# Stick-breaking attention beside seven projection slabs: the suffix sums and the value products one slab later

## What is computed

```python
z = jnp.einsum("bhqd,bhkd->bhqk", q_blk, k_blk).astype(jnp.float32) * scale
log_not = jnp.where(mask, jax.nn.log_sigmoid(-z), 0.0)
suffix = lax.cumsum(log_not, axis=3, reverse=True) - log_not
log_w = jax.nn.log_sigmoid(z) + suffix
att = jnp.where(mask, jnp.exp(log_w), 0.0)
outs.append(jnp.einsum("bhqk,bhkd->bhqd", att.astype(v.dtype), v_blk))
...
p = p + mu.astype(f32) * (prev - p)
xw = p[..., o:o + DECAY_LORA]; o += DECAY_LORA
xa = p[..., o:o + ICLR_LORA]; o += ICLR_LORA
xg = p[..., o:o + GATE_LORA]; o += GATE_LORA
log_decay = -DECAY_SCALE * jax.nn.sigmoid(w0 + jnp.tanh(xw) @ w_lora)
a = jax.nn.sigmoid(a0 + xa @ a_lora)
g = jax.nn.sigmoid(xg) @ g_lora
```

## Time and profile before

| | |
|---|---|
| median of 3 runs | 1669.34 us (1667.26 to 1671.3) |
| the profiled execution, its own time | 1670.32 us |
| its span in the trace | 1667.9 us |
| TensorE matmuls busy | 1633.1 us, 98% of the span |
| VectorE busy | 1239.9 us, 74% |
| ScalarE busy | 922.4 us, 55% |
| granted TensorE clock, mean | 0.995 of full |

### The profile page before, as it was taken

How to read it: one execution, slowest core, us unless ns; L and a number is a source line. 1 busy time by engine, 2 the same in 40 slices (tenths; PEclk the granted TensorE clock), 3 DMA queues, 4 the chain that set the end, 5 groups by cost and what they waited for, 6 DMA issues and landing times.

```text
span 1667.9 us, 29552 instructions
## 1 busy us (share of the span) xinstructions
PE 1633.1 (98%) x12590; PEld 1497.5 (90%) x12590; DVE 1239.9 (74%) x1358; ACT 922.4 (55%) x1015; POOL 37.5 (2%) x40
## 2 busy tenths in 40 slices
PE   8999999999999999999999999999999999999997
PEld 7988998999999998888999988888888897988887
DVE  6677877975788888776697787657876678677655
ACT  5376534544566557554576655448555456555445
POOL 0000000100000000000020000000000000000000
PEclk9999999999999999999999999999999998999999
DMA  8524445453454544555633455553555541445551
GB/s 295 185 90 169 160 143 202 153 206 122 158 197 181 201 161 167 202 195 187 212 133 127 165 212 188 181 198 130 201 199 189 169 177 72 167 179 184 189 187 54
DMA packets 84136, 287.14 MB, mean 172 GB/s; under 512 B 5856, under 2 KB 54112, under 8 KB 56384
## 3 DMA queue, kind: packets, MB, share of 16 engines
q1 hardware_dynamic: 79984, 273.70, 46.6%
q0 software_dynamic: 2816, 10.69, 1.8%
q10 hardware_dynamic: 1232, 1.25, 0.2%
HBM read 281.42 MB, written 4.19 MB: 171 GB/s over the span
## 4 chain that ended last, share of the span: by engine, by line
PE 86%; DVE 7%; ACT 3%; issue 1%; DMA 1%; POOL 0%; ACTq 0%; DVEq 0%; POOLq 0%
PE PS L476 86%; DVE arena L2151 2%; DVE ring_lo L2148 2%; ACT arena L1484 1%; DVE arena L2148 1%; ACT ring_hi L1484 1%; DMA arena<-spilled_gates 1%; DMA residual<-in_x_t 0%; ACT L1484 0%; ACT operand L1484 0%; DVE arena L2308 0%; DMA ring_raw<-in_w_stream 0%; DVE inv L2207 0%; DVE residual L2148 0%; PE PS L922 0%
## 5 line engine op out<-in xcount | busy, mean ns | idle before, releaser
L476 PE MATMUL PS<-operand,ring_hi 128*128 128x256 f32 (+1 forms) x4360 | 905.6, 329 | 12.7 <-DVE operand L2213 10.2
L476 PEld LDWEIGHTS PS<-operand,ring_hi 128*128 128x128 f32 x4360 | 727.6, 191 | 80.3 <-DVE ring_lo L2148 8.1
L2148 DVE TENSOR_TENSOR ring_lo<-ring_raw,ring_hi 128x2048 fp32r<-128x2048 f32 (+2 forms) x267 | 601.8, 2257 | 203.6 <-ACT ring_hi L1484 203.1
L1484 ACT ACTIVATE ring_hi<-ring_raw 128x2048 fp32r<-128x2048 f32 (+2 forms) x267 | 497.2, 1863 | 192.3 <-PE PS L476 184.7
L476 PE MATMUL PS<-operand,ring_lo 128*128 128x256 f32 x3060 | 601.9, 283 | 0.1
L476 PEld LDWEIGHTS PS<-operand,ring_lo 128*128 128x128 f32 x3060 | 479.9, 192 | 12.0 <-DVE ring_lo L2148 0.4
L1484 ACT ACTIVATE arena<-PS 128x512 f32<-128x512 f32 (+2 forms) x141 | 89.7, 642 | 175.9 <-PE PS L476 164.0
L476 PE MATMUL PS<-hidden,ring_hi 128*128 128x512 f32 x704 | 174.8, 396 | 0.0
L476 PEld LDWEIGHTS PS<-hidden,ring_hi 128*128 128x128 f32 x704 | 128.0, 188 | 26.2
L2148 DVE TENSOR_TENSOR arena<-arena,PS 128x512 f32<-128x512 f32 (+4 forms) x147 | 99.6, 683 | 28.0 <-ACT arena L1484 21.6
L1484 ACT ACTIVATE arena<-arena 128x512 f32<-128x512 f32 (+6 forms) x124 | 85.4, 702 | 59.8 <-DVE arena L2151 32.8
(11 more groups left out here) (160 smaller groups left out, 1125.0 us busy)
## 6 DMA issues: line engine op xcount, KB each, us to landing
ring_raw<-in_w_stream SPq DMA_DIRECT2D x215, 1024.0 KB, 4.8
ring_raw<-in_w_stream SPq DMA_DIRECT2D x64, 512.0 KB, 4.4
ring_raw<-in_w_stream SPq DMA_DIRECT2D x52, 256.0 KB, 3.5
spilled_gates<-arena POOLq DMA_DIRECT2D x12, 256.0 KB, 2.7
arena<-spilled_gates POOLq DMA_DIRECT2D x2, 1536.0 KB, 9.8
tables<-in_tables POOLq DMA_DIRECT2D x1, 1344.0 KB, 9.7
residual<-in_x_t ACTq DMA_DIRECT2D x4, 256.0 KB, 7.7
arena<-in_mem_t POOLq DMA_DIRECT2D x1, 1024.0 KB, 16.6
```

Of the source, the lines that this page charges most:

```text
L476: return nc.tensor.matmul(out, lhs, rhs, start=start, stop=stop, skip_group_check=True)
L1484: return nc.scalar.activation(out, in_, func, **kw)
L2148: return v.tensor_tensor(out, a, b, op)
```

## The change

On TensorE the suffix and value steps of both sets stand one slab later: scores 0, slab 0, scores 1, slab 1, slab 2, suffix 0, slab 3, suffix 1, slab 4, values 0, slab 5, values 1, slab 6. On ScalarE the exponential of set 1 moves behind shift 2 and the split of slab 6, and the operand's high half from turn j = 4 to turn j = 5, behind the split of gate slab 2. On VectorE the addition and mask of set 0 move behind shift 0, the split of slab 4 and take 2, and those of set 1 behind take 3, shift 2 and the split of slab 6. No instruction is added or removed.

```diff
             pe.wait_ge(sem("output_taken"), taken[0] - 2)
-            for j, (part, q) in enumerate(((sb_scores, 0), (sb_scores, 1), (sb_suffix, 0), (sb_suffix, 1),
+            for j, (part, q) in enumerate(((sb_scores, 0), (sb_scores, 1), (None, 0), (sb_suffix, 0), (sb_suffix, 1),
                                            (sb_values, 0), (sb_values, 1))):
-                part(q)
+                if part is not None:
+                    part(q)
                 rwkv_slab(j)
-            rwkv_slab(6)
...
             attention(0)
             shift(1)
             split_slab(START["rwkv"] + 5)
-            attention(1)
             for j in range(2, 7):
                 shift(j)
                 if j < 6:
                     split_slab(START["rwkv"] + j + 4)
-                if j == 4:
+                if j == 2:
+                    attention(1)
+                if j == 5:
                     act.wait_ge(sem("sb_y"), 1)
                     operand(XH[:, 12:16], tiles_of(0, 4))
...
             logs(1)
-            attention(0)
             shift(0)
             split_slab(START["rwkv"] + 4)
             take_rwkv(2)
-            attention(1)
+            attention(0)
             shift(1)
             split_slab(START["rwkv"] + 5)
             for j in range(3, 7):
...
                 if j < 6:
                     split_slab(START["rwkv"] + j + 3)
+                if j == 3:
+                    attention(1)
                 if j == 5:
                     dve.wait_ge(sem("sb_y"), 1)
                     operand(XL[:, 12:16], tiles_of(0, 4), XH[:, 12:16])
```

## The result

| | before | changed |
|---|---|---|
| median of 20 runs each | 1669.66 us (1667.16 to 1672.56) | 1672.8 us (1667.55 to 1674.87) |
| the profiled execution, its own time | 1670.32 us | 1672.69 us |
| its span | 1667.9 us | 1670.1 us |
| TensorE matmuls busy | 1633.1 us | 1634.5 us |

The ratio is 1.0019 (95% interval 1.0013 to 1.0026): slower by about 3.1 us, clear of noise and just inside the 0.2% that was called no change. The forecast was plus 1.15 us. The two profiled executions differ by 2.37 us, their spans by 2.2 us, and the larger part of that can be followed in the traces.

The account below looks back on a forecast made before the run. TensorE was taken as the bound, busy 1633.1 of 1667.9 us. Minus 1.82, plus 3.2, minus 0.23 made plus 1.15 us, set on the 1669.34 us median: 1670.5 us, range 1667.4 to 1673.6 us.

Parts of the forecast that it names:

- A: The forecast case: the wait moves from the suffix sums to the lora products, 1670.5 us (1670.3 to 1671.2); chance 0.60.
- B: Rival: TensorE's clock falls to half in the new wait before the lora products, 1672.9 to 1673.9 us; chance 0.22.
- The old stall: TensorE's wait before the suffix sums of set 1, for VectorE's addition of set 0: taken as gone, minus 1.82 us.
- Rival D: The addition of set 0 comes late, so the wait before the suffix sums isn't removed: up to 1672.3 us; chance 0.06.
- The queue of ScalarE: The operand's activation behind gate slab 2's split delays the lora products: TensorE waits 3.2 us instead of 0.23 us.
- The lora transfer: The lora weights' load on GpSimd's queue, released by VectorE's subtraction: taken as hidden, 0.35 us as upper end.
- the argument against B: The 1.82 us stall at 107.86 us left the clock at full, and dense work stands on both sides.
- B's price: Loss at half clock: 3.4 us for up to 6.8 us at half rate, 2.4 us if only through the lora products.
- The sum behind the lora products: Later chains each start about 1.1 us later; nothing takes the delay up or adds to it.
- The term of A: The sum of the stall removed and the lora wait added, at full clock: plus 1.15 us.
- Rival C: The gain stays, by a shorter path to the lora products or later slack: TensorE keeps 1.82 us, 1667.5 us; chance 0.12.

Follow-up runs that it names:

- e1: The changed kernel, but ScalarE makes the operand's high half in turn 5 ahead of the split of gate slab 2: 1667.23 us, ratio 0.9983.
- e2: The kernel before, with only the operand's high half moved on ScalarE from turn 4 to turn 5, behind the split of gate slab 2: 1675.91 us.
- e4: The changed kernel, but GpSimd loads the lora weights early, when slab 5 is multiplied: 1674.28 us, ratio 1.0028.
- e8: The kernel before, with only shift 6 on ScalarE moved ahead of the split of gate slab 2: 1667.28 us, ratio 0.9992.
- e9: The changed kernel measured once more, nothing altered: 1671.41 us, ratio to before 1.0015.
- e11: A repeat of e5, nothing altered: 1665.18 us, ratio to before 0.9977.
- e10: A repeat of e1, nothing altered: 1667.54 us, ratio to before 0.9993.
- e6: The changed kernel, but TensorE multiplies the first half of gate slab 1 in the wait before the lora products: 1669.65 us, ratio 1.0003.
- e5: The kernel of e1, with shift 6 on ScalarE also moved ahead of the split of gate slab 2: 1665.04 us, ratio to before 0.9975.
- e7: The kernel of e1 plus 13 unused matmuls of 64 columns between gate slab 0 and the lora products: 1670.57 us, ratio to before 1.0012.
- e3: The changed kernel plus 13 unused matmuls of 512 columns between gate slab 0 and the waits before the lora products: 1673.65 us, ratio 1.0025.

## Why the prediction was right, and where it wasn't

The time came out as no change and inside the stated range, but not by the case that set it: A ended at 1671.2 us, the median is 1672.8 us, and what happened is B. With a ratio of 1.0019 against a border at 1.002, "no change" was close to luck.

**The old stall.** Right: VectorE's addition ended at 113.18 us (forecast 113.46), TensorE came to the sums at 113.52 us (113.75), and the wait is gone. Rival D is out. Slab 6 ended near 140.29 us (the split behind it starts at 140.39 us, and 0.10 us lay between them before), 0.17 us ahead of the forecast; e1 too gains 2.06 us and not 1.82. Where the 0.2 us come from wasn't followed.

**The queue of ScalarE.** Right in mechanism and size: 3.2 us forecast, 3.21 us measured, and the lora products 8.97 us behind slab 6, forecast 8.98. e1 and e2 show it from both sides: taking the one move back removes the wait, making it alone brings it.

**The lora transfer.** Right that it doesn't decide, by e4, though the trace names it.

**The choice between A and B.** Wrong. A, with the clock at full, had 0.60 and set the predicted time; B had 0.22. The step that failed is the argument against B, that the single stall of 1.82 us had left the clock at full and that dense work stands on both sides: a wait of 3.21 us brought the fall in four profiles of four. The stall of 1.82 us left the clock at full in three of three (before, e2, e8), as the prediction read it, but it was no measure for a wait nearly twice as long. The Trainium skill, "TensorE: Matmul & The Clock Gate", section "HAM oscillation — how this bites in real kernels", says that a long enough wait for data puts the array back to half clock. The four profiles agree with it.

B's price, 2.4 to 3.4 us forecast, was narrower than what came: 1.55 us in the two profiles of the changed kernel, 4.6 us in e2 and, counted in the same way, 5.6 us in e4 (149.09 to 165.36 us). Its lower end was also worked out wrongly. 4.76 us is what the lora products take at full clock; in e4, where the clock is at half all through them, they take 8.73 us (149.09 to 157.82), 4.0 us more and not 2.4.

**The sum behind the lora products.** "Nothing takes the delay up or adds to it" can't be upheld. The term of A, plus 1.15 us forecast and 0.98 us measured at the lora start, becomes plus 2.53 us with the clock's 1.55 us and plus 2.00 us behind the break in gate slab 5, and the spans end 2.2 us apart. But the breaks belong to the single execution: e9, the same kernel with the same wait and the same fall, took 1669.52 us in its profiled execution, less than the profiled one of before. The prediction left the breaks out, and they can differ by nearly as much as the term that it worked out: 0.64 and 0.48 us in the one profile of the changed kernel, 0.15 us and none in the other.

The medians are 3.1 us apart, more than the two traces show. The recorded clocks say where the rest may lie: the mean granted clock of the 20 executions of the changed kernel averages 0.9933, that of e9's 0.9940, that of before in the rounds of e1 to e11 0.9952 to 0.9956, that of e1 and e10 0.9953 and 0.9952. That is 0.002 lower; 0.002 of 1670 us is about 3.3 us lost, or about 7 us at half clock (an estimate from these means, where each clock is recorded to 0.001), twice the 3.4 us that the two profiles show. So the fall is probably longer in many executions, as it was in e2 and e4 behind the same wait. In the changed kernel the one at 0.998 took 1667.55 us and those at 0.992 took 1673.45 to 1674.17 us; but in e9 one at 0.997 took 1670.83 us, so the clock isn't the whole spread, and where in the span it fell in each isn't recorded.

**Rival C** had asked whether the gain could stay. Not with this order of ScalarE's queue; with the order of e1 it does.

## What to carry to other kernels

When a group of steps moves in the order of one engine, write out for each other engine what now stands ahead of the moved instruction, and what that one waits for: here one activation of 1 us went behind a split that waits for the last slab, and held up VectorE's queue, the shift and the sigmoid for the next products. A wait of TensorE has to be priced with the clock behind it, which can cost more than the wait. A wait that is only filled comes back at the next instruction that hangs on the same late event (e6); make the event early instead (e1, e5). And two profiles are to be compared from a mark that both share: absolute times of one stretch differed by up to 3 us here (88.94 to 91.92 us at the same matmul) before anything was changed.

## What the runs showed of the hardware that wasn't expected

- Behind a wait of the same 3.21 us the clock stayed at half for 3.4 us in the two profiles of the changed kernel, 10.2 us in e2 and 13.6 us in e4. In e4 it fell in the wait, in the others 0.6 to 1.4 us behind its end.
- TensorE breaks off in the middle of gate slab 5 with nothing in the trace to wait for, 0.15 to 2.77 us long, in all thirteen profiles behind exactly 1616 matmuls of the kernel. 13 matmuls more, 40 us ahead, put it 13 matmuls of the slab earlier and made it 1.1 us longer (e7 against e1).
- Behind the breaks of 2.77, 2.36 and 1.68 us (e3, e7, e6) the clock fell for 3.4 us; behind those of up to 1.30 us it stayed at full. It also stayed at full behind the stall of 1.82 us and behind the 2.29 us at 297.15 us in e3, so the length of the idle time alone doesn't decide.
- The 256 KB of the second lora weights landed 4.3 us after their issue before, 3.2 us in the changed kernel (3.0 us in e9) with no weight load beside them, and 6.5 us in e4 with two beside them.
